# More block pairs in both feed-forwards of a two-layer fp32 kernel, with the weight sums made ahead on GpSimd and passed through DRAM

## The chip, the cores and the metric

One NeuronCore of one Trainium2 chip runs the whole program. The metric is the time on the device in microseconds. Before the change three runs gave 1911.08, 1911.11 and 1911.13, median 1911.11.

TensorE is called PE here, VectorE DVE, ScalarE ACT, GpSimd POOL; SP is the queue that issues the DMAs.

## The reference, cut to what matters

Two transformer layers over x of 512 tokens by 1024. The first mixes an mLSTM and a dilated-window attention, the second a gated linear attention (GLA) and a sparse attention (NSA). Each ends in a feed-forward of width 2816 (22 blocks of 128); the change touches these:

```python
hf = rmsnorm(x, norm_ffn_g)
x = x + (jax.nn.silu(hf @ w_gate) * (hf @ w_up)) @ w_down
...
h = rms_norm(x, norm_ffn_pre[l])
f = (jax.nn.silu(h @ w_ffn_gate[l]) * (h @ w_ffn_up[l])) @ w_ffn_down[l]
x = x + rms_norm(f, norm_ffn_post[l])
```

Everything is fp32.

## The kernel before, in words

**Units.** `unit_order` (line 59) lists 318 units, one for each block of 128 output columns of a weight matrix. The weights of a unit (1024 x 128) are one DMA of 512 KB into one of three RAW buffers. ACT writes their rounded upper part WH, DVE (in some units POOL) the rest WL (`split`, lines 2057, 2455 and 3261). Activations have an upper and a lower part in the same way (HH and HL, AH and AL). `products` (1551) makes 8 x 3 matmuls of 512 columns: upper by upper, upper by lower, lower by upper. A unit of the last down part has 6 x 3.

**Order.** Every engine runs the same program text and keeps its own instructions (class `Order` and its children). Each engine works through its queue in order. In front of unit i `ahead` (416) puts the split of unit i + 2 and the load of unit i + 5. WH and WL have three buffers too, so a split waits until PE is done with the unit three earlier. `evict` (2616 for DVE) takes the sum out of PSUM.

**Output units, line 755.** Out units 0 to 7 end the attention of the first layer. Evicting one is, on DVE, the residual add XT + PS, then, after ACT has made AH, the lower part AL; ACT also squares XT, and POOL adds the squares up (`add_up`, 3251).

**Lead, line 456.** `ffn` (776) starts with `lead`: gate 0 and up 0 run interleaved, two k steps each in turn, then gate 1. During this the norm's factor RB is made. The second feed-forward starts with `lead_post` (489), four units (gate 0, up 0, gate 1, up 1), behind the post-norm.

**Pairs.** From block `PAIR_FROM` = 8 on (line 19), in both feed-forwards, two blocks t and t + 1 of gate, or of up, are one pair: a Strassen-like scheme in the 2 x 2 blocks (two output blocks by two halves of k, over two halves of the tokens), with 7 products instead of 8. `pair_products` (1620) makes a product as 4 x 3 matmuls of 256 columns, 84 for a pair. The seven weight operands of a pair are three raw quarters (a11, a12, a22) and four sums (s1, s2, s4, s3). DVE makes the sums in RAW (`chunk_add`, 2470: four additions of 128 x 512 per pair), ACT rounds each operand (`chunk_hi`, 2067) and DVE subtracts (`chunk_lo`, 2493). The seven activation operands ("forms") are made once for each of four m and kept in SBUF: three scalings by gain and RB (`forms_x`, 2502), four differences and sums (`forms`, 2518), ACT's rounding of 1792 columns (`forms_hi`, 2076), and the rest, 1024 columns on DVE and 768 on POOL (`forms_lo`, 2533 and 3279). All four share one scratch tile TF, so one must be finished before the next begins. `pair_keep`, `pair_held` and `pair_add` (2081, 2539, 2547) join the products; ACT's silu follows (`pair_silu`, 2091), then the product of gate and up.

**Feed-forward order.** FFN_PARTS are blocks 0 to 7, 8 to 15, 16 to 21. A part's gate and up blocks come first. The eight down units of a part are put one behind each pair of the next part. The 14 pairs of each feed-forward so always have a down unit behind them. Without pairs, in blocks 0 to 7, gate and up are plain units.

`ffn_pairs` (807) writes that order out in steps: a step is one product of a pair or half a unit. In each it puts what the other engines are to do: evictions of the pair before, the lower parts of weight operands (`pending`), the upper parts of those whose buffers are free, one of the four operations of a form per step from the third step on, with every fifth step empty:

```python
    forms = [(f, m) for m in range(4) for f in (e.forms_x, e.forms, e.forms_hi, e.forms_lo, e.none)]
```

All loads of a feed-forward stand in SP's queue one behind the other, each behind its waits.

**POOL.** Besides the squares it makes the lower weights of every second unit in the busy parts (`lo_on_pool`, 161), and for a plain gate the product silu x RB (3292).

Of the kernel before, what the change touches and what calls it, by code (L numbers as in the profile page):

```python
# [18 lines left out]
PAIR_FROM = 8  # L19
# [39 lines left out]
def unit_order():  # L59
# [6 lines left out]
    def ffn(sfx):  # L66
# [5 lines left out]
        for a, b in FFN_PARTS:  # L72
            for t in range(a, b):
                if sfx not in PAIRED or t < PAIR_FROM:
# [100 lines left out]
def pair_start(i):  # L175

    name, j = UNITS[i][:2]
    if name[-1] == "2":
        return i - j % 2 if name in ("gate2", "up2") and "2" in PAIRED and j >= PAIR_FROM else None
    return i - j % 2 if name in ("gate", "up") and "" in PAIRED and j >= PAIR_FROM else None  # L180

# [30 lines left out]
def place_raw():  # L212


    order, user, slot, before = list(range(NR)), {}, {}, {}
    for i, (name, j, k0, nk) in enumerate(UNITS):
        if name in ("if", "small2"):
            continue
        x = order.pop(0)
        order.append(x)  # L220
        slot[i], before[i] = x, user.get(x, [])
        p = pair_start(i)
        if p is None:
            user[x] = [("lo", i)]
        else:
            user[x] = [("lo", i, 4), ("lo", i, 5), ("added", i, 6)] if p == i else [("lo", p, 2), ("lo", p, 6)]
    return slot, before
# [3 lines left out]
R_SLOT, R_BEFORE = place_raw()  # L231

# [36 lines left out]
class Order:  # L269
# [37 lines left out]
    chunk_add = chunk_hi = chunk_lo = forms_x = forms = forms_hi = forms_lo = none  # L307
# [108 lines left out]
def ahead(e, i):  # L416
    if i + 2 < len(UNITS):
        e.split(i + 2)
    settle(e)
    decays_on(e)  # L420
    if i + 5 < len(UNITS):
        e.load(i + 5)

# [331 lines left out]
def attention(e):  # L755
# [16 lines left out]
    for j in range(8):  # L772
        unit(e, unit_of("out", j))

# [31 lines left out]

def ffn_pairs(e, sfx, at):
# [7 lines left out]
    chunks = [(i, c) for i in range(at + 2, beyond) for c in ([None] if pair_start(i) is None else  # L815
                                                              range(7) if pair_start(i) == i else [])]
    for i in range(at + 5, len(UNITS) if sfx else end + 5):
        e.load(i)
    forms = [(f, m) for m in range(4) for f in (e.forms_x, e.forms, e.forms_hi, e.forms_lo, e.none)]
    n_hi, n_add, pending, queue = 0, 0, [], []  # L820
    for n, (kind, i, x) in enumerate(steps):
        if kind == "pair":
# [8 lines left out]
        for what, i2, y in now:  # L831
            if what == "silu":
# [6 lines left out]
        for y in pending:  # L839
            e.chunk_lo(*y)  # L840
# [10 lines left out]
        if n > 1 and forms:  # L851
            f, m = forms.pop(0)
# [2689 lines left out]
```

## Time and profile before

| | |
|---|---|
| median of three runs | 1911.11 us |
| profiled execution, first to last instruction (its span) | 1909.1 us |
| profiled execution's own time | the page gives its span alone; the runs lie 2.0 us above it |
| PE busy | 1898.5 us, 99% |
| DVE busy | 1255.4 us, 66% |
| ACT busy | 735.3 us, 39% |
| POOL busy | 265.1 us, 14% |
| DMA | 172.77 MB, mean 90 GB/s |

PE's busy time counts overlapping, pipelined matmuls; the time that a matmul takes away from the next is read from start to start. In timelines the columns are the start in us from the span's start, the duration in us, engine, line, operation, and tiles written and read; the brackets give the engine's idle time before it and what ended it.

### The profile page before, as it was taken

To read this page: it belongs to the slowest core of one execution; us is meant where nothing else is said; L and a number is where in the kernel's file an instruction comes from. 1 tells how busy PE (TensorE), PEld (TensorE's weight loads), DVE (VectorE), ACT (ScalarE), POOL (GpSimd) and SP (SyncE) were. 2 spreads that over 40 slices of the span, in tenths; PEclk is the share of its full clock that TensorE was granted. 3 is DMA by queue.
4 is the path that set the end of the run, shared out by engine and by line. 5 is a ranking of instruction groups with operands and counts; after the bars stand their busy time and mean duration, and the time that the engine had idled before them with its cause. 6 is when DMAs were issued, how large, how long until landed. Compare 5 with 4: busy or idle time off the path is not lost.

```text
span 1909.1 us, 26308 instructions
## 1 busy us (share of the span) xinstructions
PE 1898.5 (99%) x10599; PEld 1591.0 (83%) x10599; DVE 1255.4 (66%) x1894; ACT 735.3 (39%) x1265; POOL 265.1 (14%) x156
## 2 busy tenths in 40 slices
PE   9999999999999999999999999999999999999998
PEld 7788888888888888999997778877777878899998
DVE  7777543345455748777776756766776667887874
ACT  6332322233334444344435522224444354444442
POOL 0211210111111113000004001121111133100002
PEclk9999999999999999999999999999999999999999
DMA  5322233232321323233333222322121322333332
GB/s 177 102 70 85 88 86 115 89 99 67 89 67 45 115 91 104 78 106 102 114 108 103 77 67 78 100 79 65 56 67 40 116 79 87 100 100 100 100 130 81
DMA packets 53472, 172.77 MB, mean 90 GB/s; under 512 B 5963, under 2 KB 10643, under 8 KB 53352
## 3 DMA queue, kind: packets, MB, share of 16 engines
q1 hardware_dynamic: 52912, 170.66, 28.8%
q8 instruction: 84, 1.38, 0.3%
q10 hardware_dynamic: 440, 0.44, 0.1%
q14 instruction: 36, 0.29, 0.1%
HBM read 168.86 MB, written 2.22 MB: 90 GB/s over the span
## 4 chain that ended last, share of the span: by engine, by line
PE 94%; DVE 3%; ACT 1%; POOL 1%; issue 0%; DVEq 0%
PE PS L1561 22%; PE PS L1563 22%; PE PS L1562 22%; PE PS L1637 5%; PE PS L1639 5%; PE PS L1638 5%; PE PS L1983 1%; PE PS L2005 1%; PE PS L1780 1%; PE PS L1795 1%; PE PS L1961 1%; PE PS L1841 1%; PE PS L1827 1%; PE PS L1818 1%; PE PS L1748 1%; POOL XT L3338 1%
## 5 line engine op out<-in xcount | busy, mean ns | idle before, releaser
L1561 PE MATMUL PS<-HH,WH 128*128 128x512 f32 x1124 | 444.0, 395 | 0.8 <-DVE WL L2467 0.7
L1563 PE MATMUL PS<-HH,WL 128*128 128x512 f32 x1124 | 438.0, 390 | 0.0
L1562 PE MATMUL PS<-HL,WH 128*128 128x512 f32 x1124 | 437.4, 389 | 0.0
L2064 ACT ACTIVATE WH<-RAW 128x1024 fp32r<-128x1024 f32 (+2 forms) x256 | 261.1, 1020 | 336.4 <-PE PS L1563 271.4
L2467 DVE TENSOR_TENSOR WL<-RAW,WH 128x1024 fp32r<-128x1024 f32 (+2 forms) x195 | 251.2, 1289 | 113.7 <-ACT WH L2064 112.0
L1561 PE MATMUL PS<-AH,WH 128*128 128x512 f32 x816 | 323.7, 397 | 0.0
L1563 PE MATMUL PS<-AH,WL 128*128 128x512 f32 x816 | 318.1, 390 | 0.0
L1562 PE MATMUL PS<-AL,WH 128*128 128x512 f32 x816 | 317.6, 389 | 0.0
L1561 PEld LDWEIGHTS PS<-HH,WH 128*128 128x128 f32 x1124 | 211.1, 188 | 49.7 <-issue 4.2
L1563 PEld LDWEIGHTS PS<-HH,WL 128*128 128x128 f32 x1124 | 211.0, 188 | 45.1
L1562 PEld LDWEIGHTS PS<-HL,WH 128*128 128x128 f32 x1124 | 211.2, 188 | 42.2 <-issue 0.2
L3267 POOL TENSOR_TENSOR WL<-RAW,WH 128x1024 fp32r<-128x1024 f32 (+1 forms) x61 | 139.0, 2279 | 740.1 <-ACT WH L2064 740.1
L1637 PE MATMUL PS<-AR,WH 128*128 128x256 f32 x784 | 219.6, 280 | 0.0
L1639 PE MATMUL PS<-AR,WL 128*128 128x256 f32 x784 | 218.8, 279 | 0.0
L1638 PE MATMUL PS<-AR,WH 128*128 128x256 f32 x784 | 218.8, 279 | 0.0
L1561 PEld LDWEIGHTS PS<-AH,WH 128*128 128x128 f32 x816 | 153.2, 188 | 37.1 <-issue 6.5
L1563 PEld LDWEIGHTS PS<-AH,WL 128*128 128x128 f32 x816 | 153.2, 188 | 33.0
L1562 PEld LDWEIGHTS PS<-AL,WH 128*128 128x128 f32 x816 | 153.4, 188 | 30.5 <-issue 0.5
L2613 DVE TENSOR_TENSOR AR<-PS,RB 128x512 f32<-128x512 f32 (+2 forms) x117 | 84.3, 723 | 134.5 <-PE PS L1563 128.0
L2073 ACT ACTIVATE WH<-RAW 128x512 fp32r<-128x512 f32 x196 | 119.4, 624 | 93.3 <-DVE RAW L2486 36.7
L1637 PEld LDWEIGHTS PS<-AR,WH 128*128 128x128 f32 x784 | 147.2, 188 | 1.1
L1638 PEld LDWEIGHTS PS<-AR,WH 128*128 128x128 f32 x784 | 146.7, 187 | 1.1
(360 smaller groups left out, 2260.7 us busy)
## 6 DMA issues: line engine op xcount, KB each, us to landing
RAW<-wst SPq DMA_DIRECT2D x292, 512.0 KB, 3.6
RAW<-wst SPq DMA_DIRECT2D x16, 256.0 KB, 2.6
RAW<-wst SPq DMA_DIRECT2D x8, 384.0 KB, 3.1
XT<-xT SPq DMA_DIRECT2D x3, 512.0 KB, 7.3
out<-XT SPq DMA_DIRECT2D x4, 384.0 KB, 2.5
AR<-mx SPq DMA_DIRECT2D x4, 256.0 KB, 6.2
AR<-scr SPq DMA_DIRECT2D x16, 64.0 KB, 4.3
AR<-scr SPq DMA_DIRECT2D x8, 128.0 KB, 4.8
```

Of the source, the lines that this page charges most:

```text
L1561: T.matmul(out, wh, XH[:, k, :], start=k == 0, stop=False)
L1562: T.matmul(out, wh, XL[:, k, :], start=False, stop=False)
L1563: m = T.matmul(out, wl, XH[:, k, :], start=False, stop=k == nk - 1)
L1637: T.matmul(out, wh[:, w], xh, start=m == 0, stop=False)
L1638: T.matmul(out, wh[:, w], xl, start=False, stop=False)
L1639: t = T.matmul(out, wl[:, w], xh, start=False, stop=m == 3)
L1748: t = T.transpose(PS[:, b, q * 128:(q + 1) * 128], src[:, q * 128:(q + 1) * 128], ident())
L2064: t = A.activation(whole(WH, i, n), raw(i)[:, 0:n], ACT.Copy, scale=1.0)
L2073: t = A.activation(chunk(WH, i, c), raw_chunk(i, c), ACT.Copy, scale=1.0)
L2467: t = V.tensor_tensor(whole(WL, i, n), raw(i)[:, 0:n], f(whole(WH, i, n)), ALU.subtract)
L2613: return V.tensor_tensor(dst, src, rb, ALU.mult)
L3267: t = G.tensor_tensor(whole(WL, i, n), raw(i)[:, 0:n], f(whole(WH, i, n)), ALU.subtract)
```

## The change

Six things change.

1. `PAIR_FROM` is 2 in the first feed-forward and 4 in the second. The first gets six pairs more (20 instead of 14), the second four (18). The added pairs lie in part 0 and have no down units between them.
2. The four weight sums of each of the 38 pairs are made ahead on POOL (`sum_add`) in a tile SG of two buffers: SP loads the two raw blocks (`sum_load`, two DMAs of 512 KB), POOL makes four additions of 512 columns, SP stores the result (1 MB) to a DRAM tensor `sums`. `SUMS_AHEAD` places these steps: load at unit u, s1 at u + 2, s2 and s4 at u + 3, s3 at u + 4 or 5, store at u + 5 or 6. The first feed-forward's u go from unit 17 to 92 in steps of 4, then 3, then 4; the second's from g - 8 in steps of 4, where g = 113 is the first pair's unit: from output unit 4 on through the first feed-forward.
3. `chunk_add` is gone from DVE. RAW is handled as six halves of 256 KB; each of a pair's seven operands is a DMA of its own (`load_piece`), raw ones from the weights, sums from `sums`. Loads stand in SP's queue behind the lower part that frees their place (class `Loads`).
4. The forms no longer hold RB: `forms_x` is a tensor_scalar by the gain alone. RB is put in afterwards: POOL multiplies each gate block of a pair by RB before the silu (`pair_factor`) and again after it (`pair_silu` on POOL).
5. The first feed-forward's four forms are made in `attention` behind output units 4 to 7; the second's in `ffn_pairs` from the first step on, one operation a step, or two where `PAIR_FROM` is at most 4, as here.
6. `forms_lo` is wholly on DVE, 1792 columns.

```diff
-PAIR_FROM = 8
+PAIR_FROM = {"": 2, "2": 4}
...
+SUM_AT = {"s2": 0, "s4": 512, "s1": 1024, "s3": 1536}
+def sums_ahead():
+
+    plan, g = {}, AT["gate", 2, 0]
+    ahead_of = {"": list(range(17, 41, 4)) + list(range(42, 57, 3)) + list(range(57, 93, 4)),
+                "2": list(range(g - 8 if PAIR_FROM["2"] < 6 else g, g + 64, 4))}
+    for sfx, at in ahead_of.items():
+        for first, n in zip(at, [n for n, i in enumerate(PAIRS) if UNITS[i][0] in ("gate" + sfx, "up" + sfx)]):
+            last = 6 if sfx else 5
+            for step, what in ((0, "load"), (2, "s1"), (3, "s2"), (3, "s4"), (last - 1, "s3"), (last, "store")):
+                plan.setdefault(first + step, []).append((what, n))
+    return plan
...
 def ahead(e, i):
-    if i + 2 < len(UNITS):
+    if i + 2 < len(UNITS) and pair_start(i + 2) is None:
         e.split(i + 2)
     settle(e)
     decays_on(e)
-    if i + 5 < len(UNITS):
+    if i + 5 < len(UNITS) and pair_start(i + 5) is None:
         e.load(i + 5)
+    sums_on(e, i)
...
     for j in range(8):
         unit(e, unit_of("out", j))
+        if j > 3:
+            for f in (e.forms_x, e.forms, e.forms_hi, e.forms_lo):
+                f("", j - 4)
...
-    for i in range(at + 5, len(UNITS) if sfx else end + 5):
-        e.load(i)
-    forms = [(f, m) for m in range(4) for f in (e.forms_x, e.forms, e.forms_hi, e.forms_lo, e.none)]
-    n_hi, n_add, pending, queue = 0, 0, [], []
+    loads = Loads(e, at, len(UNITS) if sfx else end + 5, chunks)
+    forms = [(f, m) for m in range(4) for f in (e.forms_x, e.forms, e.forms_hi, e.forms_lo)] if sfx else []
+    per_step = 1 if PAIR_FROM[sfx] > 4 else 2
+    n_hi, pending, queue = 0, [], []
     for n, (kind, i, x) in enumerate(steps):
+        if (x if kind == "pair" else x[0]) == 0:
+            for u in (i, i + 1) if kind == "pair" else (i,):
+                sums_on(e, u)
...
-            if what == "silu":
+            if what == "factor":
+                e.pair_factor(i2, y)
+                queue.append(("silu", i2, y))
+            elif what == "silu":
                 e.pair_silu(i2, y)
...
-            while n_add < min(n_hi + 2, len(chunks)):
-                e.chunk_add(*chunks[n_add])
-                n_add += 1
...
-        if n > 1 and forms:
-            f, m = forms.pop(0)
+        for f, m in forms[0:per_step]:
             f(sfx, m)
+        del forms[0:per_step]
...
+            def load_piece(s, i, c):
+                for key in R_BEFORE[i, c]:
+                    sp.wait_ge(*at(*key))
+                if CHUNKS[c] in SUM_AT:
+                    n, o = PAIRS.index(i), SUM_AT[CHUNKS[c]]
+                    sp.wait_ge(*at("sum", "stored", n))
+                    src = sums_d[n, :, o:o + 512]
+                else:
+                    o = 0 if CHUNKS[c] == "a11" else 512
+                    src = wst_d[i + (CHUNKS[c] == "a22"), :, o:o + 512]
+                S.dma_start(raw_chunk(i, c), src).then_inc(*raw_in[R_SLOT[i, c]].next("raw", i, c))
...
                 def scaled(dst, j, a, b):
-                    return V.scalar_tensor_tensor(out=dst, in0=XT[:, j, a:b], scalar=col(g, j), in1=RB[:, a:b],
-                                                  op0=ALU.mult, op1=ALU.mult)
+                    return V.tensor_scalar(dst, XT[:, j, a:b], col(g, j), None, ALU.mult, ALU.bypass)
...
-                t = V.tensor_tensor(TL[sfx][:, a:a + 1024], TF[:, 0:1024], f(TH[sfx][:, a:a + 1024]), ALU.subtract)
-                t.then_inc(*dve_done["ffn"].next("forms", "lo", sfx, m, 0))
+                t = V.tensor_tensor(TL[sfx][:, a:a + 1792], TF, f(TH[sfx][:, a:a + 1792]), ALU.subtract)
+                t.then_inc(*dve_done["ffn"].next("forms", "lo", sfx, m))
...
+            def pair_factor(s, i, n):
+                pool.wait_ge(*at("free", "sum", i + n))
+                pool.wait_ge(*at("free", "spread", norm_of(UNITS[i][0])))
+                t = G.tensor_tensor(GATE[n], GATE[n], RB, ALU.mult)
+                t.then_inc(*pool_done["ffn"].next("factor", i + n))
```

## Rows read from the trace of the kernel before

**Rows 1.** The page: span, and busy time of each engine.
```profile
span 1909.1 us, 26308 instructions
...
PE 1898.5 (99%) x10599; PEld 1591.0 (83%) x10599; DVE 1255.4 (66%) x1894; ACT 735.3 (39%) x1265; POOL 265.1 (14%) x156
```

**Rows 2.** The page: the chain that ended last, by engine.
```profile
PE 94%; DVE 3%; ACT 1%; POOL 1%; issue 0%; DVEq 0%
```

**Rows 3.** PE timeline: start us, us, instruction; starts of units (L1561) and a pair.
```profile
688.57 0.39 PE L1561 MATMUL PS<-AH,WH 128*128 128x512 f32 x1
...
776.51 0.28 PE L1637 MATMUL PS<-AR,WH 128*128 128x256 f32 x1
...
786.41 0.40 PE L1561 MATMUL PS<-HH,WH 128*128 128x512 f32 x1
...
1575.83 0.39 PE L1561 MATMUL PS<-HH,WH 128*128 128x512 f32 x1
...
1597.60 0.39 PE L1561 MATMUL PS<-HH,WH 128*128 128x512 f32 x1
```

**Rows 4.** DVE timeline, output units: adds (L2655), AL, weight splits (L2467).
```profile
672.45 0.69 DVE L2655 TENSOR_TENSOR XT<-XT,PS 128x512 f32<-128x512 f32 x1 [0.97 <-PE PS L1563]
673.93 0.75 DVE L2446 SCALAR_TENSOR_TENSOR AL<-XT,COL,AH 128x512 fp32r<-128x512 f32 x1 [0.79 <-ACT AH L2048]
...
680.91 1.44 DVE L2467 TENSOR_TENSOR WL<-RAW,WH 128x1024 fp32r<-128x1024 f32 x1 [0.79 <-ACT WH L2064]
...
686.35 1.45 DVE L2467 TENSOR_TENSOR WL<-RAW,WH 128x1024 fp32r<-128x1024 f32 x1 [0.79 <-ACT WH L2064]
```

**Rows 5.** DVE timeline, one form beside plain units.
```profile
715.37 0.48 DVE L2510 SCALAR_TENSOR_TENSOR AR<-XT,COL,RB 128x256 f32<-128x256 f32 x1
...
716.83 1.22 DVE L2467 TENSOR_TENSOR WL<-RAW,WH 128x1024 fp32r<-128x1024 f32 x1
717.96 0.42 DVE L2523 TENSOR_TENSOR AR<-AR,VT 128x256 f32<-128x256 f32 x1
...
719.55 0.68 DVE L2613 TENSOR_TENSOR AR<-PS,RB 128x512 f32<-128x512 f32 x1
```

**Rows 6.** Groups by line: busy us, mean ns.
```profile
L2482 DVE TENSOR_TENSOR RAW<-RAW 128x512 f32<-128x512 f32 x28 | 19.2, 685 | 0.0
...
L2078 ACT ACTIVATE AR<-AR 128x1792 fp32r<-128x1792 f32 x8 | 13.6, 1696 | 4.8 <-DVE AR L2530 4.8
L2752 DVE TENSOR_SCALAR AR<-AR 128x512 f32<-128x512 f32 x32 | 13.5, 423 | 8.7 <-ACT AR L2138 8.6
...
L2536 DVE TENSOR_TENSOR AR<-AR,AR 128x1024 fp32r<-128x1024 f32 x8 | 9.8, 1222 | 0.9 <-ACT AR L2078 0.6
```

**Rows 7.** DVE timeline: a split beside POOL; the second feed-forward's lead.
```profile
1082.39 2.31 DVE L2467 TENSOR_TENSOR WL<-RAW,WH 128x1024 fp32r<-128x1024 f32 x1
...
1584.24 0.69 DVE L2452 TENSOR_TENSOR AL<-AR,AH 128x512 fp32r<-128x512 f32 x1 [0.70 <-ACT AH L2154]
1585.26 1.23 DVE L2467 TENSOR_TENSOR WL<-RAW,WH 128x1024 fp32r<-128x1024 f32 x1 [0.33 <-ACT WH L2064]
```

**Rows 8.** POOL timeline: additions of 512 columns.
```profile
674.50 1.34 POOL L3258 TENSOR_TENSOR AR<-AR 128x512 f32<-128x512 f32 x1 [4.10 <-ACT AR L2054]
...
1081.83 1.79 POOL L3305 TENSOR_TENSOR AR<-AR 128x512 f32<-128x512 f32 x1 [39.28 <-DVE AR L2613]
```

**Rows 9.** PE timeline: the last matmul.
```profile
1903.20 0.39 PE L1712 MATMUL PS<-WH,AL 128*128 128x512 f32 x1
```

**Rows 10.** Stages: us, busy PE, PEld, DVE, ACT, POOL, PEclk, DMA share, GB/s.
```profile
60.00:210.00 150.00, 150.00 (x678) 122.67 (x677) 107.87 (x176) 46.54 (x76) 31.20 (x17) 1.00 0.29 89
1908.00:1909.10 1.10, 0.00 (x0) 0.00 (x0) 0.00 (x0) 0.00 (x0) 0.00 (x0) 0.56 0.17 61
```

**Rows 11.** The chain in order of time: its first piece.
```profile
1.47 6.82 PE PS L1539 x18
```

**Rows 12.** DVE timeline, last down units.
```profile
1025.80 2.05 DVE L2467 TENSOR_TENSOR WL<-RAW,WH 128x768 fp32r<-128x768 f32 x1
```

More of the change, by code:

```diff
@@ L231 @@
 R_SLOT, R_BEFORE = place_raw()
+PAIRS = [i for i in range(len(UNITS)) if pair_start(i) == i]
+SUM_AT = {"s2": 0, "s4": 512, "s1": 1024, "s3": 1536}
[9 more added lines that the diff above has]
+    return plan
+SUMS_AHEAD = sums_ahead()
 class Signal:
@@ L420, in ahead, with sums_on @@
     decays_on(e)
-    if i + 5 < len(UNITS):
+    if i + 5 < len(UNITS) and pair_start(i + 5) is None:
         e.load(i + 5)
+    sums_on(e, i)
+def sums_on(e, i):
+    for what, n in SUMS_AHEAD.get(i, []):
+        if what == "load":
+            e.sum_load(n)
+        elif what == "store":
+            e.sum_store(n)
+        else:
+            e.sum_add(n, what)
 def quarter(e, i, q):
@@ L804, in pair_steps, with __init__, on, lo @@
     return steps
+class Loads:
+    def __init__(self, e, at, end, chunks):
+        self.e = e
+        self.behind = {("lo", i) if c is None else ("lo", i, c) for i, c in chunks}
+        self.pieces = [(i, c) for i in range(at + 1, end) for c in (
+            ([None] if i > at + 4 else []) if pair_start(i) is None else range(7) if pair_start(i) == i else [])]
+        self.on()
+    def on(self):
+        while self.pieces and not any(x in self.behind for x in R_BEFORE.get(self.pieces[0], [])):
+            i, c = self.pieces.pop(0)
+            if c is None:
+                self.e.load(i)
+            else:
+                self.e.load_piece(i, c)
+    def lo(self, chunks):
+        for i, c in chunks:
+            self.e.chunk_lo(i, c)
+            self.behind.discard(("lo", i) if c is None else ("lo", i, c))
+            self.on()
 def ffn_pairs(e, sfx, at):
@@ L856, in ffn_pairs @@
             if len(x) == 6:
-                for y in pending:
-                    e.chunk_lo(*y)
+                loads.lo(pending)
                 pending = []
@@ L869, in ffn_pairs @@
                 e.pair_add(i, x - 5)
-                queue.append(("silu" if gate else "hi", i, x - 5))
-    for y in pending:
-        e.chunk_lo(*y)
+                queue.append(("factor" if gate else "hi", i, x - 5))
+    loads.lo(pending)
     for y in chunks[n_hi:]:
         e.chunk_hi(*y)
-        e.chunk_lo(*y)
+        loads.lo([y])
 def last(e):
@@ L1155, in build @@
         RC = sb("RC", [128, 16])
+        SG = sb("SG", [128, 2, 2048])
         reached = {}
@@ L2091, in pair_silu @@
             def pair_silu(s, i, n):
-                act.wait_ge(*at("free", "sum", i + n))
+                act.wait_ge(*at("factor", i + n))
                 x = GATE[n]
@@ L3277, in chunk_lo, with sum_add, pair_silu @@
                 t.then_inc(*weight_lo_pool.next("lo", i, c))
[L3279 to L3284 removed]
+            def sum_add(s, n, what):
+                g = SG[:, n % 2, :]
+                s2, s4, s1, s3 = (g[:, o:o + 512] for o in (0, 512, 1024, 1536))
+                if what == "s1":
+                    pool.wait_ge(*at("sum", "raw", n, 0))
+                    pool.wait_ge(*at("sum", "raw", n, 1))
+                    t = G.tensor_tensor(s1, s1, s3, ALU.add)
+                elif what == "s2":
+                    pool.wait_ge(*at("sum", "s1", n))
+                    t = G.tensor_tensor(s2, s2, s1, ALU.subtract)
+                else:
+                    pool.wait_ge(*at("sum", "s2", n))
+                    x = s4 if what == "s4" else s3
+                    t = G.tensor_tensor(x, x, s2, ALU.add)
+                t.then_inc(*pool_done["sums"].next("sum", what, n))
+            def pair_factor(s, i, n):
[3 more added lines that the diff above has]
+                t.then_inc(*pool_done["ffn"].next("factor", i + n))
+            def pair_silu(s, i, n):
+                pool.wait_ge(*at("silu", i + n))
+                t = G.tensor_tensor(GATE[n], GATE[n], RB, ALU.mult)
+                t.then_inc(*pool_done["ffn"].next("silu2", i + n))
             def after(s, i, p):
```

106 lines of the change are left out of this document (49 added, 57 removed).

## The prediction

> **What bounds the kernel now.** I read the page's busy shares first, then the chain that ended last, then TensorE's (PE's) timeline at the places that the change touches, and last VectorE's (DVE's), ScalarE's (ACT's) and GpSimd's (POOL's) there. The shares show PE busy for 1898.5 of 1909.1 us [rows 1], and PE is 94% of the chain [rows 2]: nearly every microsecond is a matmul, so a change pays by the matmul time that it takes away and costs whatever PE waits. In the timeline a pair (84 matmuls of 256 columns) runs from 776.51 to 786.41, 9.90 us; four plain units run from 1575.83 to 1597.60, 5.44 us each [rows 3]. Two units are 10.88 us, so a pair saves 0.98 us.
>
> The profiled span is 1909.1 us and the median run 1911.1, so 2.0 us lie around the span. I sum against the span and add these 2.0.
>
> **Term 1, matmul work.** The first feed-forward pairs blocks 2 to 7 too: 3 block pairs, gate and up, 6 pairs. The second pairs 4 to 7: 4 pairs. 10 x 0.98 = 9.8 us less on PE.
>
> **Term 2, forms during the output units.** The forms of the first feed-forward (the seven combinations of the activations) were made beside plain units 0 to 7. Now they are queued on DVE behind the evictions of output units 4 to 7, ahead of the next units' weight splits. DVE runs in order, so I walk its queue. Let S be the start of the residual add of output unit 4, 672.45. The AL subtraction starts at S + 1.48 and DVE can go on 0.67 later, at S + 2.15 [rows 4]. The three scalings took 716.83 - 715.37 = 1.46 us start to start, the four subtractions and additions 719.55 - 717.96 = 1.59 [rows 5]. Then DVE waits for ACT's rounding, 1.70 us, and some 0.1 of semaphores; then it subtracts 1792 columns, which POOL no longer shares: 1024 took 1.22 and 512 0.69, so about 2.0, 1.95 start to start [rows 6]. Then the weight split of 1024 columns, 1.15 start to start (1.23 long, [rows 7]). Sum: 2.15 + 1.46 + 1.59 + 1.8 + 1.95 + 1.15 = 10.1 us where a unit lasts 5.44. The residual adds come at 682.6, 692.7 and 702.8 instead of 677.9, 683.3 and 688.8.
> The low weights of gate 0 follow the second of these forms: before they were ready at 682.35, now at 692.8, and PE wants them at 688.57 [rows 3, 4]. Those of up 0 were ready at 687.8, now at 702.9; the lead takes up 0 right after six matmuls of gate 0, at about 690.0. That is 12.9 us of wait. Gate 1's follow one step later, at 713.1, and PE gets there at 703.0 + 10.4 = 713.4: no more. I take 13.0 (12 to 14.5: what the 6.2 us of head start of gate 0's weights hide is already out of it).
>
> A choice stands in the scalings: they become a tensor_scalar with one SBUF tensor. A tensor_scalar of 512 columns took 0.42 us where a two-tensor operation took 0.69 [rows 6]; halved to 256 columns that makes 0.75 us for the three instead of 1.46. The Trainium skill, "VectorE: DVE Perf Modes", section on mode 2x_2P, says that a one-source fp32 operation within SBUF reads through both ports; by it the term would be 0.7 us less per form. Here POOL's square sum runs from 674.50 to 675.84 [rows 8], just where they would start, and may hold them up by as much; so I take no gain in this term, and half of it in term 3.
>
> **Term 3, forms of the second feed-forward, two per half unit.** DVE ends the lead's last subtraction at 1584.24 + 0.60 = 1584.85, 9 us behind PE, which began the first unit behind the lead at 1575.83; the first pair is now due at 1597.60 [rows 3, 7]. Between them stand four forms (1.46 + 1.59 + 1.95 = 5.0 each, plus 1.8 of wait for ACT less the split that one step lets in between), two whole weight splits (2.3), four half ones (2.4) and the evictions of three units (one operation of 0.69, or two with a wait for ACT between: 0.6, 2.0 and 0.6 start to start). Walked in order: gate 3's weights at 1589.0 against 1586.7, up 3's at 1596.5, the last low form at 1615.7. The pair starts 18.1 us late; with the shorter scalings (0.7 x 4) 15.3. I take 16.7. Nothing covers it, for before the forms had eight units, 43.5 us, and now four.
>
> **Term 4, the clock.** The last matmul started at 1903.20, and over 1908.0 to 1909.1 the granted clock reads 0.56, most of it at the lower level, 1.2 GHz; before, it was at the upper one, 2.4 GHz [rows 9, 10]. So it fell within 5 us of idle PE. Terms 2 and 3 each hold a longer idle stretch (8.8 and 13.7 us). What comes behind runs at half speed for a while; the kernel's own start took 6.82 us for 18 matmuls that take 2.1 us later [rows 11], so at most 4.7 us each, at least nothing. I take 2 each, 4.
>
> **Term 5, sums on POOL.** 38 pairs x 4 additions of 512 columns. POOL's addition took 1.34 us alone [rows 8], so 204 us go to POOL. They also cost DVE: at 1082.39 a split that takes 1.23 alone took 2.31, with a POOL addition running to 1083.62 [rows 7, 8]: the split waited it out. So each POOL addition may hold DVE up to 1.3 us. Place by place:
> - Units 17 to 92 (mLSTM and attention, 80 additions): DVE 108 and POOL 31 of 150 us [rows 10]; six sums make that 139 in the worst case. PE's weights are split two units, some 11 us, ahead. 0 to 5 us, I take 1.
> - The second feed-forward's sums start at output unit 4; three additions meet the forms of term 2: 0 to 3.9, I take 1.3.
> - Back-to-back pairs in the first feed-forward: per two pairs (19.8 us) POOL gets 4 additions and 4 multiplications by the norm's factor, 10.4 us; DVE's two-tensor work is 14 chunk splits, two products and two subtractions at 0.60, 10.8 us. Excluding each other they ask 21.2 us. What DVE is rid of, 4 additions of 0.685 per pair [rows 6], is less than POOL's. 0 to 6, I take 1.
> - The last eight down units, 4.08 us each: the split of 768 columns already takes 2.05 us beside the square sums on POOL [rows 12], and seven more additions come in between, up to 9.1 us, in a stretch where DVE and POOL both already wait for each other. Some of it meets POOL's idle time. 0 to 6, I take 3.
>
> **What costs nothing.** Factor, silu and second product of a gate (two POOL operations of 1.3 us and one of ACT between) lie in the 9.9 us of the up pair. SP's loads by chunk wait for splits 8 us ahead of use; sum stores wait for POOL and stand in SP's queue behind loads that were due earlier. DMA: 2.75 MB more per pair, 105 MB, is 55 GB/s on average over 89 at a share of 0.29 [rows 10]; only in the back-to-back pairs (1.84 MB in 9.9 us and 2.1 in 19.8, 292 GB/s) does it come near full by that ratio, which the 0 to 6 above covers.
>
> **Sum.** -9.8 + 13.0 + 16.7 + 4 + (1 + 1.3 + 1 + 3) = +30.2; span 1939.3, time 1941.3. Low ends: -9.8 + 12 + 15.3 = +17.5, 1928.6. High ends: -9.8 + 14.5 + 18.1 + 9.4 + 5 + 3.9 + 6 + 6 = +53.1, 1964.2.
>
> **Rivals.** A difference of 0.2% (3.8 us) is about what a measurement tells from none.
> A: PE never waits; forms and weights are in time. For it speaks that PE is 99% busy with four forms made beside plain units already, and DVE only 66% [rows 1]; against it, the walk of the queue, in which 7 us of DVE's own work stand in each 5.44. It decides if a form costs DVE under 1.6 us beyond its present unit. 1911.1 - 9.8 = 1901.3. Chance 0.10.
> B: only one of the two starts bites, or each by a few microseconds, for the waits for ACT overlap more than I let them: -9.8 plus 5 to 18, 1906 to 1920. Chance 0.13, of which 0.03 ends faster and 0.04 level.
> C: POOL's additions cost far more than the places above: each of the 152 holds back a DVE operation that feeds PE. Were a fifth of them on the path, 30 x 1.3 = 39 us instead of 6.3: 1974. For it speaks the 2.31 us split; against it the two units of head start in attention. The skill's "SBUF — State Buffer", section Who interferes with whom, calls the shared port pair an exclusive lock held for the whole instruction, and the 2.31 us agree. Chance 0.08.
> My forecast: 0.69.
>
> **Range and chances.** Forecast and C are slower, with most of B. Faster 0.13, same 0.04, slower 0.83. The range is 1913 to 1957: it leaves out A (0.10), the lower two fifths of B (0.05) and somewhat over half of C (0.05).
>
> **What would show it.** Right: 20 + 18 pairs of 9.90 us; PE idle 10 us or more in the lead of the first feed-forward, ended by a DVE weight split, and 10 or more before the first pair of the second, ended by a DVE form; granted clock at half behind both; output units' residual adds 10 us apart; POOL busy for over 450 us. Wrong: those two gaps under 3 us, or DVE splits at 1.23 beside POOL additions. Were the time under 1911, terms 2 and 3 would both have failed.

## The result, and the profile after

The changed kernel takes 1966.78 us (median of four runs, 1966.2 to 1967.61) beside 1911.12 of the kernel before: ratio 1.0292, 95% interval 1.0277 to 1.0306. It is slower by 55.7 us where the forecast was 30.2, and it lies above the range of 1913 to 1957. The profiled execution has a span of 1965.5 us against 1909.1 [rows 1].

The page after, the span and the busy times:

```profile
span 1965.5 us, 27705 instructions
PE 1905.4 (97%) x10959; PEld 1608.0 (82%) x10959; DVE 1328.3 (68%) x1872; ACT 753.5 (38%) x1325; POOL 576.1 (29%) x366
```

and its chain by engine, with the groups of instructions that the next sections speak of:

```profile
PE 78%; DVE 10%; issue 4%; ACT 4%; POOL 4%; DMA 1%; DVEq 0%; SPq 0%; ACTq 0%; POOLq 0%
...
L1728 PE MATMUL PS<-AR,WH 128*128 128x256 f32 x1064 | 302.6, 284 | 24.1 <-DVE AR L2602 9.2
...
L1653 PE MATMUL PS<-AH,WH 128*128 128x512 f32 x720 | 288.3, 400 | 18.2 <-DVE WL L2558 11.7
...
L2567 DVE TENSOR_TENSOR WL<-RAW,WH 128x512 fp32r<-128x512 f32 x266 | 244.9, 953 | 46.2 <-ACT WH L2164 44.7
```

In the chain PE has fallen from 94% [rows 2] to 78%: a fifth of the span now hangs on what other engines do. The products of pairs (L1728) waited 24.1 us and plain products (L1653) 18.2. A weight split of a pair's operand (L2567, 512 columns) takes 953 ns in the mean. In the kernel before, the same splits took 692:

```profile
L2499 DVE TENSOR_TENSOR WL<-RAW,WH 128x512 fp32r<-128x512 f32 x196 | 128.5, 692 | 1.6 <-ACT WH L2073 1.2
```

**Where the 56.4 us of span went.** From the starts of PE's product matmuls I took, stage by stage, the time beyond 0.2267 us for a matmul of 512 columns and 0.1178 for one of 256 (their spacing when nothing is waited for) as idle, and inside the stretches of half clock up to as much again as clock. The difference to the kernel before, beside what the prediction had:

| stage (after, us from the start) | idle added | forecast |
|---|---|---|
| start of the kernel, to 27 | 0.7 | 0 |
| mLSTM and attention, to 640 | 0.8 | 1 |
| lead and plain blocks of the first feed-forward, 640 to 734.65 | 18.4 | 14.3 (13.0 + 1.3) |
| pairs of blocks 2 to 7, 734.65 to 812.02 | 15.2 | 1 |
| pairs of blocks 8 to 21, to 1023.2 | 1.4 | 0 |
| down units, to 1076 | 2.6 | 3 |
| second feed-forward, 1557 on | 16.4 | 16.7 |
| lower clock, all stretches | 10.7 | 4 |
| ten more pairs | -9.8 | -9.8 |
| sum | 56.4 | 30.2 |

The change puts nothing into the first 27 us: in the traces of the other runs that row is -0.1 to 0.4.

A pair did cost what was forecast: in the kernel that starts both at block 6 (below) the two pairs of blocks 6 and 7 lasted 20.67 us with 0.88 of idle in them, twice 9.90.

Two of the big waits are where the prediction put them. PE's waits after, 640 to 735 us, and then 1560 to 1697 us:

```profile
PE PS L1653 <- DVE WL L2558: 9.9, 1, 9.9
PE PS L1653 <- issue: 6.0, 1, 6.0
...
```

```profile
PE PS L1728 <- DVE AR L2602: 9.2, 2, 7.0
PE PS L1653 <- DVE WL L2558: 5.0, 3, 2.3
```

The 6.0 us shown as "issue" lie in front of gate 0's first matmul. It reads the weights whose split (L2558) began at 696.19 and ended at 697.41, and it started at 697.51. The 9.9 us come six matmuls later, in front of up 0's first. The 9.2 us are the last low forms (L2602). The third big loss, in the pairs of blocks 2 to 7, is the surprise. The waits of all engines, 685 to 815 us, read:

```profile
DVE WL L2567 <- ACT WH L2164: 20.5, 8, 6.2
ACT AR L2185 <- POOL AR L3366: 19.7, 5, 5.9
...
PE PS L1728 <- DVE WL L2567: 7.2, 3, 3.3
```

DVE's splits wait for ACT's rounding (L2164), and ACT stands at a silu (L2185) that waits for the gate's factor on POOL (L3366). One round of it, POOL's timeline:

```profile
772.62 1.68 POOL L3366 TENSOR_TENSOR AR<-AR,RB 128x512 f32<-128x512 f32 x1 [12.78 <-DVE AR L2624]
774.26 1.75 POOL L3353 TENSOR_TENSOR SG<-SG 128x512 f32<-128x512 f32 x1
776.09 1.62 POOL L3356 TENSOR_TENSOR SG<-SG 128x512 f32<-128x512 f32 x1
777.80 1.29 POOL L3360 TENSOR_TENSOR SG<-SG 128x512 f32<-128x512 f32 x1
779.05 1.29 POOL L3371 TENSOR_TENSOR AR<-AR,RB 128x512 f32<-128x512 f32 x1
780.30 1.28 POOL L3366 TENSOR_TENSOR AR<-AR,RB 128x512 f32<-128x512 f32 x1
```

ACT's and DVE's beside it:

```profile
775.39 0.36 ACT L2179 ACTIVATE AR<-PS 128x256 f32<-128x256 f32 x1
781.61 0.63 ACT L2185 ACTIVATE AR<-AR 128x512 f32<-128x512 f32 x1 [5.86 <-POOL AR L3366]
782.15 2.69 ACT L2164 ACTIVATE WH<-RAW 128x512 fp32r<-128x512 f32 x5
```

```profile
774.12 0.73 DVE L2567 TENSOR_TENSOR WL<-RAW,WH 128x512 fp32r<-128x512 f32 x1
775.52 1.04 DVE L2567 TENSOR_TENSOR WL<-RAW,WH 128x512 fp32r<-128x512 f32 x1 [0.67 <-ACT WH L2164]
782.79 3.63 DVE L2567 TENSOR_TENSOR WL<-RAW,WH 128x512 fp32r<-128x512 f32 x3 [6.23 <-ACT WH L2164]
```

The factor of a gate pair's first half stands ahead of three additions for the second feed-forward (SG), that of the second half behind them. ACT waits 5.86 us for it with five roundings of weights behind it in its queue, which then come in a row; DVE waits 6.23 for the first of them, and of the 44 splits in this stretch 13 lie beside a POOL operation and take 1.05 to 1.78 us, where most take 0.68 or 0.69. PE stood 3.1 us at 781. The pattern repeats every 25.2 us (747.28, 772.62, 797.84), where two pairs are 19.8.

### The profile page after: what moved, and what is told of

Same layout as the page of the kernel before. It is cut to its first block, busy times and chain, and to the rows that moved or that the text cites. A ratio compares the mean times of both kernels' runs of the same rounds, so it can differ in the third digit from the quotient of the medians.

```text
span 1965.5 us, 27705 instructions
## 1 busy us (share of the span) xinstructions
PE 1905.4 (97%) x10959; PEld 1608.0 (82%) x10959; DVE 1328.3 (68%) x1872; ACT 753.5 (38%) x1325; POOL 576.1 (29%) x366
## 2 busy tenths in 40 slices
DMA packets 97256, 282.45 MB, mean 144 GB/s; under 512 B 10827, under 2 KB 15507, under 8 KB 92264
## 4 chain that ended last, share of the span: by engine, by line
PE 78%; DVE 10%; issue 4%; ACT 4%; POOL 4%; DMA 1%; DVEq 0%; SPq 0%; ACTq 0%; POOLq 0%
PE PS L1653 18%; PE PS L1655 17%; PE PS L1654 17%; PE PS L1728 4%; PE PS L1730 4%; PE PS L1729 4%; DVE WL L2558 1%; DVE WL L2567 1%; PE PS L2074 1%; PE PS L2096 1%; PE PS L1871 1%; PE PS L1886 1%; PE PS L2052 1%; POOL AR L3366 1%; PE PS L1932 1%
## 5 line engine op out<-in xcount | busy, mean ns | idle before, releaser
L1653 PE MATMUL PS<-HH,WH 128*128 128x512 f32 x1060 | 420.2, 396 | 8.1 <-DVE WL L2558 6.4
L1654 PE MATMUL PS<-HL,WH 128*128 128x512 f32 x1060 | 413.1, 390 | 0.0
L1728 PE MATMUL PS<-AR,WH 128*128 128x256 f32 x1064 | 302.6, 284 | 24.1 <-DVE AR L2602 9.2
L1653 PE MATMUL PS<-AH,WH 128*128 128x512 f32 x720 | 288.3, 400 | 18.2 <-DVE WL L2558 11.7
L1730 PE MATMUL PS<-AR,WL 128*128 128x256 f32 x1064 | 299.3, 281 | 0.0
L1729 PE MATMUL PS<-AR,WH 128*128 128x256 f32 x1064 | 299.2, 281 | 0.0
L2558 DVE TENSOR_TENSOR WL<-RAW,WH 128x1024 fp32r<-128x1024 f32 (+2 forms) x175 | 231.6, 1324 | 93.2 <-ACT WH L2155 91.8
L1655 PE MATMUL PS<-AH,WL 128*128 128x512 f32 x720 | 282.1, 392 | 0.0
L1654 PE MATMUL PS<-AL,WH 128*128 128x512 f32 x720 | 281.8, 391 | 0.0
L2567 DVE TENSOR_TENSOR WL<-RAW,WH 128x512 fp32r<-128x512 f32 x266 | 244.9, 953 | 46.2 <-ACT WH L2164 44.7
L1653 PEld LDWEIGHTS PS<-HH,WH 128*128 128x128 f32 x1060 | 199.4, 188 | 56.2 <-issue 9.7
L1728 PEld LDWEIGHTS PS<-AR,WH 128*128 128x128 f32 x1064 | 202.4, 190 | 29.8 <-DVE AR L2602 9.7
L1729 PEld LDWEIGHTS PS<-AR,WH 128*128 128x128 f32 x1064 | 202.0, 190 | 1.0
L1730 PEld LDWEIGHTS PS<-AR,WL 128*128 128x128 f32 x1064 | 202.5, 190 | 0.0
L2164 ACT ACTIVATE WH<-RAW 128x512 fp32r<-128x512 f32 x266 | 155.9, 620 | 66.0 <-DMA RAW<-wst 38.3
L1653 PEld LDWEIGHTS PS<-AH,WH 128*128 128x128 f32 x720 | 136.0, 189 | 53.3 <-issue 24.9
```

Source lines behind the costliest of these rows:

```text
L1653: T.matmul(out, wh, XH[:, k, :], start=k == 0, stop=False)
L1654: T.matmul(out, wh, XL[:, k, :], start=False, stop=False)
L1655: m = T.matmul(out, wl, XH[:, k, :], start=False, stop=k == nk - 1)
L1728: T.matmul(out, wh[:, w], xh, start=m == 0, stop=False)
L1729: T.matmul(out, wh[:, w], xl, start=False, stop=False)
L1730: t = T.matmul(out, wl[:, w], xh, start=False, stop=m == 3)
```

## The experiments

Theories for the pairs of blocks 2 to 7 were (1) the order in POOL's and ACT's queues, (2) exclusion between DVE and POOL and (3) DMA traffic.

**1. The additions behind the factor.**

```diff
-        if (x if kind == "pair" else x[0]) == 0:
+        if (x == 2 if kind == "pair" else x[0] == 0):
```

> Edit: within the pairs, the weight sums (loads, additions, stores) of a step are issued two chunk products later, so that on POOL the three additions stand behind the second half's factor and second product instead of ahead of them. Nothing else moves; the number of additions, transfers and bytes is the same. Theory 1 (order): in the back-to-back pairs of blocks 2 to 7, 77.4 us long where six pairs of 9.90 are 59.4, ScalarE waits 5.9 us for a factor that stands behind three additions on POOL, and its weight roundings stand behind that wait. Then this edit takes most of the 18.0 us away: stretch from the first pair to block 8 under 64 us, time 1950 to 1956. Theory 2 (work of the shared port: DVE's splits and POOL's 512-column operations exclude each other) and theory 3 (the DMA traffic of sums and pieces): the work is the same, so the stretch stays over 74 us and the time at 1963 to 1968.

Measured: 1964.17 us (1962.96 to 1967.33), ratio 1.0283 (1.0266 to 1.0300), by the times no different from the changed kernel. The stretch fell from 77.4 to 70.4 us. ACT's wait for the factor fell from 19.7 to 2.7 us and the two stretches of half clock there are gone, but what DVE and the pieces cost is not: PE still waited 8.3 us for DVE there, 1.0 of it for a split and 7.3 for evictions that stand in DVE's queue with the splits, and ACT waited 11.1 us for pieces of sums. This run's row of windows for that stretch (length; busy time of PE, PEld, DVE, ACT and POOL; clock; DMA share; GB/s):

```profile
734.00:804.35 70.35, 61.79 (x505) 59.50 (x505) 59.54 (x80) 31.30 (x60) 38.32 (x26) 1.00 0.72 246
```

and its group of splits in it:

```profile
L2567 DVE TENSOR_TENSOR WL<-RAW,WH 128x512 fp32r<-128x512 f32 x44 | 43.7, 1026 | 9.5 <-ACT WH L2164 9.5
```

PE's longest waits in the stretch:

```profile
PE PS L1728 <- DVE AR L2610: 4.3, 3, 1.7
PE PS L1728 <- DVE VT L2624: 1.5, 2, 0.7
PE PS L1728 <- DVE VT L2629: 1.5, 2, 0.8
```

So theory 1 holds for 7 of the 18 us and falls as the only cause. Later the edit gave half of it back: blocks 8 to 21 took 214.7 us, not 211.1.

**2. The second feed-forward's sums from block 8 on.**

```diff
-                "2": list(range(g - 8 if PAIR_FROM["2"] < 6 else g, g + 64, 4))}
+                "2": list(range(g + 12, g + 84, 4))}
```

> Edit: the second feed-forward's sums start 20 units later, at block 8 of the first feed-forward: none of them meets output units 4 to 7, the plain blocks 0 and 1 or the pairs of blocks 2 to 7 any more; their number is the same. Theory 1 (order), 2 (port) and 3 (DMA) all expect the stretch of the pairs of blocks 2 to 7 to fall from 77.4 to about 60 us; read against the run before this one it tells how much of it the order alone explains. New here: the three scalings of a form, tensor_scalar operations of 256, 256 and 512 columns, took 4.1 us beside POOL's additions and 0.8 to 1.2 us in the second feed-forward without them. If each short DVE operation waits out a POOL operation, the forms behind output units 4 to 7 lose 2 to 3 us each, the two waits of PE in the first feed-forward's lead (6.2 and 10.3 us) fall by 5 us together, and the time comes to 1941 to 1947. If the forms are long for another reason, the two waits stay and the time is 1948 to 1951.

Measured: 1949.41 us (1947.58 to 1949.49), ratio 1.0198 (1.0183 to 1.0213). That is above the 1941 to 1947 of the theory and inside the 1948 to 1951 that were to speak for another reason. The two waits in the lead decide: they did not stay, as that other reading wanted, but fell by 3.1 us together, not by 5. The stretch, as windows and as the group of splits:

```profile
730.35:791.57 61.22, 59.76 (x505) 59.09 (x505) 49.97 (x80) 31.52 (x60) 17.93 (x12) 1.00 0.58 179
```

```profile
L2567 DVE TENSOR_TENSOR WL<-RAW,WH 128x512 fp32r<-128x512 f32 x44 | 33.0, 779 | 9.5 <-ACT WH L2164 9.5
```

Against the run before this one it is 9.1 us shorter, and the same 44 splits take 10.7 us less of DVE (43.7 - 33.0): without the additions, what is left of the loss goes together with the longer splits, and in run 1 all but 0.4 us of PE's waits were for DVE. That speaks for exclusion, theory 2, in addition to theory 1. The 9.1 us are between two runs that also differ in the additions' transfers, which the next run puts back.

The forms behind the output units show the price of one meeting. DVE in the changed kernel, one form:

```profile
687.70 1.38 DVE L2577 TENSOR_SCALAR AR<-XT,COL 128x256 f32<-128x256 f32 x1
689.00 1.38 DVE L2577 TENSOR_SCALAR VT<-XT,COL 128x256 f32<-128x256 f32 x1
690.29 0.47 DVE L2577 TENSOR_SCALAR AR<-XT,COL 128x512 f32<-128x512 f32 x1
```

and POOL beside it:

```profile
687.59 1.33 POOL L3324 TENSOR_TENSOR AR<-AR 128x512 f32<-128x512 f32 x1 [9.41 <-ACT AR L2145]
688.88 1.33 POOL L3353 TENSOR_TENSOR SG<-SG 128x512 f32<-128x512 f32 x1
```

and DVE in the run with the sums from block 8 on, where only the square sum is left on POOL:

```profile
687.02 1.38 DVE L2577 TENSOR_SCALAR AR<-XT,COL 128x256 f32<-128x256 f32 x1
688.33 0.34 DVE L2577 TENSOR_SCALAR VT<-XT,COL 128x256 f32<-128x256 f32 x1
688.59 0.47 DVE L2577 TENSOR_SCALAR AR<-XT,COL 128x512 f32<-128x512 f32 x1
```

A scaling that takes 0.34 us lasts 1.38 next to a POOL operation of 1.33. (The first scaling is long in both runs, for it meets the square sum in both.) The output units' residual adds are 10.7 us apart here and 11.8 and 12.8 in the changed kernel (685.64, 697.41, 710.20 on its chain). PE's two waits come to 5.2 and 8.3 us between matmul starts instead of 6.2 and 10.3.

**3. Additions of 8 columns.**

```diff
-                s2, s4, s1, s3 = (g[:, o:o + 512] for o in (0, 512, 1024, 1536))
+                s2, s4, s1, s3 = (g[:, o:o + (8 if UNITS[PAIRS[n]][0][-1] == "2" else 512)] for o in (0, 512, 1024, 1536))
```

> Edit: the additions of the second feed-forward's sums take 8 columns instead of 512, so the output leaves these sums out; transfers, order and waits are the same. Theory 1 (order) and theory 2 (port): the stretch of the pairs of blocks 2 to 7 falls from 77.4 to under 63 us. Theory 3 (DMA): it stays above 74 us. Time by 1 or 2: 1943 to 1953, as the forms behind the output units lose their meeting with the additions too; by 3: over 1960.

The edit leaves out all but 8 of the 512 columns of these sums. Measured, in a single run: 1944.34 us, and the stretch 61.7 us at a higher rate of transfer than the changed kernel's 225 GB/s there:

```profile
730.56:792.23 61.67, 59.87 (x504) 58.75 (x504) 51.45 (x80) 31.40 (x60) 23.38 (x26) 1.00 0.83 279
```

The group of splits in it:

```profile
L2567 DVE TENSOR_TENSOR WL<-RAW,WH 128x512 fp32r<-128x512 f32 x44 | 34.8, 822 | 8.9 <-ACT WH L2164 8.9
```

With every byte and every wait in place 2.3 us of the 18.0 are left, against 1.8 in run 2. The DMA engines were busy 83%; ACT waited 9.3 us for pieces to land, never over 2.6, and PE lost next to nothing by it: theory 3 falls for this stretch. The length of the additions on POOL is what costs, by the order (run 1) and by the splits beside them.

**4. Loads twice.**

```diff
                 for x in (0, 1):
                     d = S.dma_start(SG[:, n % 2, 1024 * x:1024 * x + 1024], wst_d[PAIRS[n] + x, :, :])
+                    if UNITS[PAIRS[n]][0][-1] == "2":
+                        d.then_inc(*sum_in[n % 2].next("sum", "once", n, x))
+                        sp.wait_ge(*at("sum", "once", n, x))
+                        d = S.dma_start(SG[:, n % 2, 1024 * x:1024 * x + 1024], wst_d[PAIRS[n] + x, :, :])
```

> Edit: the raw weights from which the second feed-forward's sums are made are loaded twice, one load after the other: 1 MB more per pair, 18 MB in all, and SyncE's queue waits for the first one to land (3 to 5 us). Theory 3 (the DMA engines are full in the back-to-back pairs, 226 GB/s on average there): the stretch of blocks 2 to 7 grows from 77.4 us by 3 MB at about 380 GB/s, 8 us or more, and the time to over 1974. Theories 1 and 2: it grows by less than 3 us unless SyncE's waits hold up pieces.

Measured, in a single run: 2049.95 us, 83.2 more. The stretch of blocks 2 to 7 grew by 13.9, blocks 8 to 21 by 63.7. SP stood 150.9 us at the new waits:

```profile
SPq L1557 <- DMA SG<-wst: 150.9, 36, 5.3
```

Bytes and waits were both doubled here, so this run alone tells nothing between them; the next adds the bytes alone.

**5. Stores twice.** The same number of bytes more, without a new wait on SP.

```diff
+                if UNITS[PAIRS[n]][0][-1] == "2":
+                    d = S.dma_start(sums_d[len(PAIRS) + n, :, :], SG[:, n % 2, :])
+                    d.then_inc(*sum_out[n % 2].next("sum", "twice", n))
```

> Edit: each sum of the second feed-forward is stored twice, the second copy to a place nobody reads: 1 MB more written per pair, 18 MB in all, as many bytes as the doubled loads brought, but SyncE's queue waits for nothing new. The doubled loads cost 83 us (4.6 us for each of 18, about the 5 us that SyncE stood waiting for a load to land). Theory a (SyncE's queue: what stands behind a wait there comes late): time within 10 us of the changed kernel's, under 1977. Theory b (bytes: the DMA engines are the limit beside pairs): the same growth as the doubled loads, over 2020; halfway would be 2000.

Measured, in a single run: 1983.52 us, 16.7 more: a fifth of what the doubled loads cost, between the two theories and nearer to the first. The stretch of blocks 2 to 7 did not grow (77.4). Blocks 8 to 21 did, by 16.1 us, where the engines moved

```profile
811.40:1038.60 227.20, 216.96 (x1488) 199.84 (x1489) 177.29 (x222) 86.95 (x150) 108.39 (x68) 0.99 0.81 283
```

283 GB/s instead of 257. The raw pieces of 256 KB landed in a median of 6.8 us there instead of 5.8, and ACT waited 92.6 us for raw weights instead of 42.7. So the transfers do begin to cost there. Not all of it need be bytes: the wait that SP has before it loads SG again, for the store to be done, grew from 4.9 to 13.3 us in these blocks. And a wait at the head of SP's queue costs more, though reads and writes may differ in price by themselves.

**6. The second feed-forward from block 6**, on top of run 2; `per_step` is then 1.

```diff
-PAIR_FROM = {"": 2, "2": 4}
+PAIR_FROM = {"": 2, "2": 6}
```

> Edit, on top of the kernel whose sums start at block 8: the second feed-forward's pairs start at block 6 instead of 4, and its forms are issued one per half unit instead of two. Theory (term 3 of the prediction): the waits of PE before and in its first pair (7.0 and 10.5 us idle, 4.3 us of half clock in the run before this) go, and the two pairs less cost 2 us: time 1949.4 - 20 + 2 = 1931 (1928 to 1935). Rival (the pairs of blocks 4 to 7 lose time for their own sake, as those of blocks 2 to 7 did): the waits move to block 6 and over half of them stay, time over 1940.

Measured, in a single run: 1943.14 us, outside the range: the rival's sign. From 1540 us on idle is 10.7 and clock 2.1, where run 2 had 18.0 and 4.3. One wait is left before block 6, and the form ends it:

```profile
PE PS L1728 <- DVE AR L2602: 6.8, 1, 6.8
```

Sixteen operations at one per half unit of 2.72 us take 43.5 us. DVE ends the lead's work some 9 us behind PE, and counted from there block 6 was due after 34.5.

**7. The first feed-forward from block 6**, on top of run 2.

```diff
-PAIR_FROM = {"": 2, "2": 4}
+PAIR_FROM = {"": 6, "2": 4}
...
         unit(e, unit_of("out", j))
-        if j > 3:
-            for f in (e.forms_x, e.forms, e.forms_hi, e.forms_lo):
-                f("", j - 4)
...
-    forms = [(f, m) for m in range(4) for f in (e.forms_x, e.forms, e.forms_hi, e.forms_lo)] if sfx else []
+    forms = [(f, m) for m in range(4) for f in (e.forms_x, e.forms, e.forms_hi, e.forms_lo)]
```

> Edit, on top of the kernel whose sums start at block 8: the first feed-forward's pairs start at block 6 instead of 2, and its forms are taken from behind the output units and issued one per half unit beside blocks 1 to 5. Theory (term 2 of the prediction): the 14.9 us of idle PE in the lead and 3.2 us of half clock go, and the 2.6 us in the pairs of blocks 2 to 7 shrink to under 1; four pairs less cost 3.9 us: time 1949.4 - 20 + 3.9 = 1933 (1931 to 1937). Rival (DVE has no room for the forms beside plain units in either place): PE waits over 5 us before the first pair and the time is over 1940.

Measured, in a single run: 1932.82 us, as expected. From 640 us to the first pair 0.8 us of idle is left, as in the kernel before, and no half clock: term 2 is the place of the forms.

**8. Both from block 6**: the edits of runs 1, 2 and 7, with

```diff
+PAIR_FROM = {"": 6, "2": 6}
```

> Edit: both feed-forwards in pairs from block 6, forms one per half unit beside the plain blocks of both, the second's sums from block 8 of the first on and issued two chunk products late. Theory: nothing of terms 2 and 3 is left, four pairs more than in the kernel before save 3.9 us, and the sums' meetings with DVE in mLSTM, attention and the down units give back 1 to 4 us: 1908 to 1912, level with the kernel before or 0.1% faster. Rival (sums and their 105 MB cost by themselves, wherever they stand): over 1915.

Measured: 1931.92 us (1928.27 to 1932.39), ratio 1.0104 (1.0087 to 1.0121), far off. It has run 6's wait of 6.8 us again with 2.1 of clock, and it lost 5.3 us of idle in blocks 8 to 21 and 4.5 of idle and clock in the down units, where run 7 had 1.2 and 2.1. The 5.3 go with the later issue of the sums (run 1 lost 5.0 there with the same edit). The 4.5 need not: run 6, without that edit, lost 4.2 in the down units too, and the cause of this was not tried.

**9. Both from block 6, the second's forms two per half unit, its sums beside GLA.** As run 8 without the edit of run 1, and

```diff
-                "2": list(range(g + 12, g + 84, 4))}
+                "2": list(range(g + 68, g + 136, 4))}
...
-    per_step = 1 if PAIR_FROM[sfx] > 4 else 2
+    per_step = 2 if sfx else 1
```

> Edit: both feed-forwards in pairs from block 6, the first's forms one per half unit and the second's two per half unit; the second's sums are made beside gated linear attention and what follows it, behind the last down unit, and are issued at once. Theory (the 6.8 us wait for the last low form in the run before this one is only the pace of issue: 16 operations at one per half unit are 43.5 us from the lead's end, where block 6 is due after 34.5; at two per half unit DVE needs 31 us): the wait is under 1 us and no half clock follows it; with the sums away from the down units the stalls there go too. Time 1911.1 - 3.9 (four pairs) + 0.8 (mLSTM, attention) + 1 to 2 = 1908 to 1911. Rival (DVE has no room for the forms in eight plain units of the second feed-forward at any pace): wait over 4 us and time over 1915.

Measured: 1930.78 us (1928.44 to 1931.24), ratio 1.0100 (1.0083 to 1.0117). The rival was nearer. No pair waits for a form, but PE idles 10.2 us beside the forms (1.5 in the kernel before) and loses 3.2 to the clock. From the last down unit to the first pair of the second feed-forward it takes 603.8 us where the next run takes 595.2. Of that, the sums beside GLA cost 8.8 us here and 1.2 there.

**10. The same with the sums from block 8 on**, `range(g + 12, g + 84, 4)` again.

> The same as the run before it, but with the second feed-forward's sums from block 8 of the first on, across its pairs and down units. Theory: 3 to 6 us more than there, in the pairs of blocks 8 to 21 (1.5 us) and in the last down units (2.7 us): 1912 to 1916. If it is level with it (within 1 us), where the sums stand no longer matters once they are away from the back-to-back pairs and the forms.

Measured: 1926.02 us (1925.6 to 1927.8), ratio 1.0081 (1.0066 to 1.0096). It is 4.8 us faster than run 9, not slower: the sums cost 3.2 us in the down units and 1.2 at GLA's start, less than the 8.8 beside GLA. The loss in the second feed-forward is as there, within 1 us.

**11. Sums alone**, the second's forms still two per half unit.

```diff
-PAIR_FROM = {"": 6, "2": 6}
+PAIR_FROM = {"": 8, "2": 8}
```

> Edit: pairs from block 8 in both, as in the kernel before; what is left of the change is that the sums are made ahead on POOL (the second's from block 8 of the first on), go through DRAM and are loaded by piece, and that the gate's factor is on POOL. It costs the sums alone. Theory (term 5, apart from the back-to-back pairs): 0.8 us in mLSTM and attention, 1.5 in the pairs of blocks 8 to 21, 2.7 in the down units: 1914 to 1917. Rival (they cost nothing where DVE has head start): 1910 to 1912.

Measured: 1926.7 us (1925.05 to 1926.77), ratio 1.0080 (1.0065 to 1.0095), where neither theory was. The early stages cost what was expected or less: 0.8 us to gate 0, 0.3 in the pairs (1.5 expected), 2.6 in the down units. The rest is the second feed-forward, though no pair waited there. PE's waits from 1560 to 1650 us:

```profile
PE PS L1650 <- DVE WL L2555: 8.4, 5, 2.3
```

These are the whole splits of plain units, late behind two form operations per half unit.

**12. The same, one form operation per half unit.**

```diff
-    per_step = 2 if sfx else 1
+    per_step = 1
```

> The kernel of the run before this one (pairs from block 8 in both, sums ahead), with the second feed-forward's forms one per half unit again, as in the kernel before, instead of two. In that run PE idled 10.2 us beside the forms and lost 3.1 to the lower clock though no pair was waiting, all of it ended by DVE's whole weight splits at 1590 to 1615 us; before, it was 1.5 us in the same units. Theory (two forms' operations per half unit are more than DVE can do there, whatever block the pairs start at, and the sums cost 3.8 us: 0.8 in mLSTM and attention, 1.0 in the pairs, 2.0 in the down units): 1926.7 - 11.8 = 1914.9 (1913 to 1917). Rival (the sums' stores and loads or the one-source scalings cost in the second feed-forward, not the pace): over 1920.

Measured: 1917.25 us (1916.92 to 1919.41), ratio 1.0035 (1.0022 to 1.0049), just above the range. PE's waits there:

```profile
PE PS L1650 <- DVE WL L2555: 2.0, 5, 0.7
```

The pace cost 9.5 us. What is left, 6.2, is the price of sums made ahead: 0.7 to gate 0, 0.3 in the pairs, 2.7 in the down units and 2.5 beside the second feed-forward's forms, which now have no share on POOL and no empty step between them; which of these two it is was not tried. No version run here beats the kernel before.

## Why the prediction was wrong

The direction, the two starts and most of their size were right. The time lies 10 us above the range, and above the sum of the forecast's own high ends, 1964.2, too. Of the 26.2 us between forecast and span, 14.2 are the pairs of blocks 2 to 7, 6.7 the clock and 4.1 the first feed-forward's lead.

**Term 1** held: 9.90 us a pair, 9.8 in all.

**Term 2** took 6.2 + 10.3 = 16.5 us for the 13.0 forecast. Without additions near it (run 2) it is 13.4, with steps of 10.7 us for the 10.1 walked: the term was right, and what was too small is "its meeting with the forms at output units", taken at 1.3 and worth 3.1. One addition met the second form and two the third, and each held DVE up by 1.0 us of its 1.3, where the forecast took a third of 1.3. Another wait, of 1.1 us, lies ahead of gate 0.

**Term 3** was forecast at 16.7 and came to 16.4 of idle. The walk had the last low form 18.1 us behind the due time of the pair, and it ended 18.2 behind it (1655.33, where 1637.15 was due). But it is not one wait before the first pair: 5.0 lie at plain units before it, 2.2 and 7.0 inside its first product, and the pair starts only 7 us late. So the near match of the size is in part luck. The choice of half the gain for the shorter scalings held: the three take 1.04 us from start to start (1640.85 to 1641.89) where they took 1.46, 0.42 less and not 0.7. The cause that term 3 gave, one wait for all forms, was half the story: runs 9 to 12 show that two operations per half unit cost 9.5 us through the plain units' splits even where pairs start at 8. Starting at 6 therefore cures little: at that pace the plain units wait, at half the pace the pair does.

**Term 4, the clock,** was forecast at 4 and came to 10.7, beyond its upper end of 9.4. The granted clock, stretches of the changed kernel:

```profile
695.00:715.00 20.00, 7.55 (x17) 5.58 (x18) 16.55 (x18) 5.29 (x7) 6.69 (x6) 0.50 0.22 79
753.00:756.30 3.30, 3.30 (x18) 3.30 (x17) 0.74 (x1) 0.16 (x1) 3.10 (x3) 0.50 1.01 377
783.70:787.00 3.30, 2.81 (x13) 2.81 (x14) 3.30 (x5) 1.14 (x3) 1.57 (x1) 0.50 0.29 87
1637.00:1640.30 3.30, 3.30 (x9) 2.62 (x8) 2.60 (x3) 0.72 (x2) 0.00 (x0) 0.50 0.53 159
1647.30:1660.80 13.50, 6.42 (x28) 6.13 (x29) 11.18 (x18) 6.46 (x10) 1.30 (x1) 0.50 0.24 78
```

The two long ones cost 3.6 and 2.7 us, where 2 was taken for each. The other 4.4 are three short stretches behind idle pieces of only 2 to 3 us, which the forecast, with one stretch for each long wait, did not have. The length of a wait does not tell by itself: behind the 3.4 us at 805.8, longer than any of these three, the clock stayed at its upper level.

**Term 5** failed at its third place, and this is the step that broke the forecast: "Back-to-back pairs in the first feed-forward ... 0 to 6, I take 1". It was 15.2 of idle and 2.8 of clock, 18.0 together. Run 1 took 7.0 us of it by order alone (the clock among them) and run 2 another 9.1. The estimate set 21.2 us of operations against 19.8, as if the two engines could take turns at will. It left out that POOL works in order, so the factor can stand behind three additions, that ACT's next roundings stand behind the silu that wants it, and that POOL's eight operations then come in one run of 12.6 us. In that run DVE first stands 6.2 us with nothing rounded to split, and then its splits fall beside POOL's operations, three of them in 3.63 us. With this place fell the sentence in "what costs nothing" that factor, silu and second product lie in the 9.9 us of the up pair: the work does, its place in two queues does not. The other places held: 0.8 for 1, and 4.0 for the down units and the pairs before them where 3 was taken.

**Bytes.** "DMA comes near full" in those pairs was no cause: run 3 moved 279 GB/s there and lost 2.3 us. The whole traffic grew by 109.7 MB (172.77 to 282.45), where the forecast had 105.

**Rivals.** A and B fell with the waits of 10.3 and 7.0 us. C came nearest in time (1974) and had the right engine. Its count, one addition in five on the path, was too high: they cost 3.1 at the forms, 16.2 between the back-to-back pairs (with the clock), 4.0 behind them and 0.8 in mLSTM and attention, 24.1 us, which is 18 to 19 times 1.3, one in eight.

**Not settled.** Run 1 moved loads and stores with the additions, so the 7.0 us is for the step as a whole. Exclusion rests on the longer splits and on PE's waits for DVE; no run kept the additions long and put them where DVE has nothing to do. And of run 4's cost, how much is SP's waits and how much reads in place of writes was not tried.

## What to carry to other kernels

When work moves to an engine that seemed idle, write down what stands behind it in that engine's queue, who waits for that, and what stands behind the waiter; a busy sum of both engines bounds none of this. Side work goes where the next engine has head start: 80 additions cost 0.8 us beside units split 11 us ahead, while 15 cost 16 us between back-to-back pairs. And preparation with a deadline (forms) has both a due time and a pace, and each can be the limit.

## What the runs showed of the hardware

A DVE scaling of 256 columns next to a POOL operation lasted 1.38 us against 0.34 alone, so here a short DVE operation waits for POOL's to end and takes four times as long. The Trainium skill, "SBUF — State Buffer", section Who interferes with whom, has the port pair locked for a whole instruction, and these rows agree. The granted clock fell to half, at 753 and 784 us, also where PE's longest waits had been 2.0 us (at 749) and 3.1 us (at 781), but not behind 3.4 us at 805.8. SP's queue is a resource of its own: 36 waits of 4.2 us in it, with 18 MB more loaded, cost 83 us, where 18 MB more stored without a new wait cost 16.7, each in a single run.
